# End of the first embedding: the first row tile turned by halves of its columns, two of its low parts ahead of the third gated product

## What is computed

```python
gate = jax.nn.sigmoid(rms_norm(h, g_ple[i]) @ ple_w_gate[i])      # p0: the embedding, i = 0
h = h + gate * (p[i] @ ple_w_proj[i])
h = h + FFN_HALF * swiglu(rms_norm(h, g_ffn1[i]), ffn1_w_in[i], ffn1_w_out[i])   # f2: i = 1
```

## Time and profile before

| | us |
|---|---|
| median of 3 runs | 1303.97 |
| lowest to highest | 1303.74 to 1305.53 |
| profiled execution, its own time | 1304.07 |
| its span on the core | 1302.3 |

### The profile page before, as it was taken

The page is one execution under the profiler, slowest core; times in us unless marked ns, Lnnn a source line. Parts: engine busy times, 40 slices in busy tenths (PEclk is TensorE's granted clock), DMA queues, the critical chain, the costliest instruction groups (busy, mean ns, idle before and its releaser), DMA issues.

```text
span 1302.3 us, 16738 instructions
## 1 busy us (share of the span) xinstructions
PE 1285.5 (99%) x6242; PEld 1058.6 (81%) x6242; DVE 929.1 (71%) x1295; ACT 678.7 (52%) x973; POOL 126.9 (10%) x190
## 2 busy tenths in 40 slices
PE   9999999999999999999999999999999999999997
PEld 6888888888888888888887777888888887788886
DVE  6878948986678956677875577667895656655674
ACT  6444537756444546644445567644444735566542
POOL 2000003712000000000001230000000133200000
PEclk9999999999999999999999999999999999999999
DMA  9765645228665554666564643466564496445541
GB/s 299 227 193 193 204 147 187 81 77 261 196 194 194 195 192 162 194 191 195 191 199 151 238 162 114 154 193 194 194 225 151 173 282 224 158 137 178 174 149 33
DMA packets 148673, 236.29 MB, mean 181 GB/s; under 512 B 10016, under 2 KB 103376, under 8 KB 148096
## 3 DMA queue, kind: packets, MB, share of 16 engines
q1 hardware_dynamic: 143600, 222.26, 52.4%
q0 software_dynamic: 4640, 12.81, 3.3%
q10 hardware_dynamic: 368, 0.37, 0.1%
HBM read 233.27 MB, written 4.47 MB: 183 GB/s over the span
## 4 chain that ended last, share of the span: by engine, by line
PE 91%; DVE 4%; ACT 3%; issue 1%; DMA 1%; SPq 0%; POOL 0%; POOLq 0%; DVEq 0%; ACTq 0%
PE acc L619 20%; PE acc L621 20%; PE acc L620 20%; PE acc L652 7%; PE acc L656 7%; PE acc L653 7%; PE misc L695 4%; DVE wl L2017 1%; ACT wh L1484 1%; PE misc L1289 1%; PE misc L836 1%; PE misc L1145 1%; DMA raw<-in_ffn_w_in_dram 1%; ACT xh L1528 0%; PE acc L816 0%
## 5 line engine op out<-in xcount | busy, mean ns | idle before, releaser
L2017 DVE TENSOR_TENSOR wl<-raw,wh 128x2048 fp32r<-128x2048 f32 (+2 forms) x200 | 452.7, 2270 | 183.4 <-ACT wh L1484 182.4
L1484 ACT ACTIVATE wh<-raw 128x2048 fp32r<-128x2048 f32 (+2 forms) x206 | 385.4, 1894 | 124.1 <-PE acc L656 104.3
L619 PE MATMUL acc<-wh,xh 128*128 128x512 f32 (+1 forms) x832 | 325.4, 391 | 2.6 <-ACT qf L1867 0.9
L621 PE MATMUL acc<-wh,xl 128*128 128x512 f32 (+1 forms) x832 | 322.9, 388 | 0.0
L620 PE MATMUL acc<-wl,xh 128*128 128x512 f32 (+1 forms) x832 | 322.7, 388 | 0.0
L619 PEld LDWEIGHTS acc<-wh,xh 128*128 128x128 f32 x832 | 156.3, 188 | 37.7 <-DVE wl L2005 3.2
L621 PEld LDWEIGHTS acc<-wh,xl 128*128 128x128 f32 x832 | 156.3, 188 | 31.9
L620 PEld LDWEIGHTS acc<-wl,xh 128*128 128x128 f32 x832 | 156.3, 188 | 31.1
L1567 ACT ACTIVATE sg<-acc,rstd 128x256 f32<-128x256 f32 x88 | 41.4, 475 | 242.7 <-PE acc L621 242.6
L2185 DVE STREAM_TRANSPOSE aT<-a_n 32x384 f32<-32x384 f32 (+1 forms) x256 | 137.2, 536 | 3.9
L652 PE MATMUL acc<-wh,ah 128*128 128x512 f32 x320 | 125.0, 391 | 0.0
(11 more groups left out here) (365 smaller groups left out, 1610.6 us busy)
## 6 DMA issues: line engine op xcount, KB each, us to landing
raw<-in_ffn_w_in_dram SPq DMA_DIRECT2D x172, 512.0 KB, 4.8
raw<-in_ffn_w_out_dram SPq DMA_DIRECT2D x88, 512.0 KB, 4.3
raw<-in_w_in_dram SPq DMA_DIRECT2D x64, 512.0 KB, 4.8
raw<-in_fox_w_in_dram SPq DMA_DIRECT2D x24, 512.0 KB, 4.3
raw<-in_ple_w_gate_dram SPq DMA_DIRECT2D x16, 512.0 KB, 4.2
raw<-in_mla_w_o_dram SPq DMA_DIRECT2D x8, 512.0 KB, 4.4
raw<-in_fox_w_o_dram SPq DMA_DIRECT2D x8, 512.0 KB, 4.4
raw<-in_w_out_dram SPq DMA_DIRECT2D x8, 512.0 KB, 4.4
```

The costliest lines, as they stand in the source:

```text
L619: pe.matmul(dst, hi, rhs_h, start=first, stop=False)
L621: return pe.matmul(dst, lo, rhs_h, start=False, stop=last)
L1484: act.activation(wh[:, s, 0:n], raw[:, s, 0:n], ACT.Copy).then_inc(hi_done, 1)
L2017: dve.tensor_tensor(wl[:, s, 0:n], raw[:, s, 0:n], wh[:, s, 0:n].bitcast(F32), ALU.subtract)\
```

## The change

Norm 4 (n4) takes the placing of n8 (k // 4 picks the bank). PE turns tile 0 of n4 by halves: the first half ahead of the last trio of the projection, waiting for the first quarter's sum alone (`h_half`, which p0's embed(0,0) now raises too), the second half behind that trio. Tile 1 is turned ahead of trio k = 7 in place of 6, by halves one straight after the other. DVE makes low parts 0 and 1 of tile 0 ahead of embed(1,0), the other six behind it. p1 counts `h_half` one further; its order is as before.

```diff
-            return (2 * t + k // 4, k % 4) if r == 8 else (2 * t + k % 2, k // 2)
+            return (2 * t + k // 4, k % 4) if r in (4, 8) else (2 * t + k % 2, k // 2)
...
-        TURN_AT = {"n1": 4}
+        TURN_AT = {"n1": 4, "n4": 7}
...
             def x_wait(name):
                 rd = PLAN[name][3]
-                return lambda t, k: pe.wait_ge(m_read[2 * t + k % 2], rd[2 * t + k % 2] + k // 2 + 1)
+                def wait(t, k):
+                    b, i = place(4 if name == "n4" else 0, k, t)
+                    pe.wait_ge(m_read[b], rd[b] + i + 1)
+                return wait
...
                         if t == 0 and k == TURN_AT.get(name, DK - 2):
                             rows_ready(pe, r, 1)
-                            turn_rows(name, 1)
+                            if name == "n4":
+                                turn_half(name, 1, 0)
+                                turn_half(name, 1, 1)
+                            else:
+                                turn_rows(name, 1)
...
                         for k in range(2):
-                            if t + n + k == 3 and after == "n8":
-                                pe.wait_ge(h_half, 1)
+                            if t + n + k == 3:
+                                pe.wait_ge(h_half, 1 if name == "p0" else 2)
                                 turn_half(after, 0, 0)
-                            elif t + n + k == 3:
-                                turn_h(after, r_after)()
...
             ple("p0", "n3", 3, "n4", 4)
+            rows_ready(pe, 4, 0)
+            turn_half("n4", 0, 1)
             ffn("f2", "n4", 4, "n5", 5)
...
-                    pe.wait_ge(h_half, 2)
+                    pe.wait_ge(h_half, 3)
                     turn_half("n8", 1, 0)
...
                     if n:
                         e.then_inc(h_added, 1)
-                    elif name == "p1":
+                    elif t == 0 or name == "p1":
                         e.then_inc(h_half, 1)
...
                 embed(0, 0)
                 embed(0, 1)
+                if after != "n8":
+                    rest_x(after, r + 1, 0, 0, 0)
+                    rest_x(after, r + 1, 0, 1, 1)
                 embed(1, 0)
...
                 else:
-                    rest(after, r + 1, 0)
+                    for k in range(2, DK):
+                        rest_x(after, r + 1, 0, k, k)
                     embed(1, 1)
                     rest(after, r + 1, 1)
```

## The result

| | before | changed |
|---|---|---|
| median of 14 runs, us | 1303.94 | 1307.26 |
| profiled execution | 1304.07 | 1307.26 |
| its span | 1302.3 | 1305.4 |

The ratio is 1.0025, with a 95% interval of 1.0018 to 1.0032: slower by 3.3 us. The forecast was 1307.3 us, with a range of 1305.9 to 1308.3.

The account below looks back on a forecast made before the run. PE's list of products plus its holes bounds the kernel. Head holes -0.88 us against 4.2 us of new holes and paced trios give +3.36: 1307.43 profiled, 0.10 less for the median, 1307.3 us; range 1305.9 to 1308.3.

Parts of the forecast that it names:

- The gain at the head: PE's holes of 0.58 us before turning tile 0 and 0.30 us before f2's first trio: at most 0.88 us gained.
- the first sum's cover of 0.81: Gated sum of columns 0 to 511 of tile 0 is done 0.81 us before PE wants to turn.
- The extra passage from transposes to products: Turning tile 0 by halves adds one more switch on PE from transposes to products, costing about 0.1 us.
- The round trip: ACT's high part and DVE's low part alternating over one misc bank: 0.79 us a step, against PE's 0.68.
- DVE's third sum: Tile 1's first-half sum between low parts 1 and 2 puts low part 2 at 516.20; fourth sum 2.2 us later.
- ACT between the tiles: Weights' high part, tile 0's square and its read-out put high part 0 of tile 1 at 522.42, before 520.43.
- The weights: Low part of f2's third weight group, behind tile 1's low parts, ends at 530.37; chunk 1 at 530.52, +3.4 us.
- Behind chunk 1: After chunk 1 of f2: later weights covered again, other waits cost nothing; nothing different but the shift.
- Rival 1: High and low parts keep their 0.39 us a step, so not slower: -0.35, 1303.6 us; chance 0.04.
- Rival 2: DVE reaches the third weight group 1.3 us sooner, so tile 1's fill ends last: +2.05, 1306.0 us; chance 0.12.
- Rival 3: PE's clock falls to its lower level in a hole: 5.4 us more for a tile's products, 1312.7; chance 0.03.
- Rival 4: Halves come no earlier, PE's first-half wait being on a count that comes with the second: +4.3, 1308.3; chance 0.02.

Follow-up runs that it names:

- the run with the order taken back: Changed kernel with DVE's third gated sum again ahead of all low parts of tile 0, halves and new banks kept: median 1306.90 us.
- the kernel with four banks: Changed kernel with k = 0 to 3 alternating between banks 0 and 1, k = 4 to 7 between banks 2 and 3: median 1303.27 us.

## Why the prediction was right

**The gain at the head** came a little larger: trio 0 at 514.30, forecast 514.5; the first sum's cover of 0.81 was real. "These 0.88 us are all that this change can give" counts holes only. Trio 0 came 0.98 earlier, because the two groups of four transposes and the trio between them took 1.54 us in all (512.76 to 514.30), where the eight and the trio had taken 1.62 (513.36 to 514.98). The extra passage from transposes to products, put at 0.1, shows no cost. It made no difference, as trio 2 waits for low part 2 in any case.

**The round trip** of 0.79 us held within 0.01 in every one of the steps over one bank, in both tiles (tile 0: 513.80, 514.59; 518.00, 518.79, 519.58; tile 1: 522.67, 523.46, 524.25, 525.03; 526.08, 526.86, 527.65), and the step at which the bank changes took 0.26, as forecast. It was the number on which all hung. Eleven round trips stand in the chain, five in tile 0 and six in tile 1, not the ten by which the lower bound was reckoned: that bound should have been 0.1 lower.

**DVE's third sum** put low part 2 at 516.18 (forecast 516.20) and, with the trips behind it, low part 7 at 519.58 (519.62) and the turning of tile 1 at 521.31 (521.34). The holes of PE were as forecast, 0.78 for 0.8 and 1.10 for 1.1.

**ACT between the tiles** was 0.14 off: high part 0 of tile 1 at 522.28, forecast 522.42. The term that I mis-sized is the read-out of the squares: ACT goes on 0.09 behind its start, not 0.19, which is its duration. The trace of before has this too: there the read-out of tile 1 starts at 524.26, and the next instruction at 524.36. The other 0.04 had come from tile 0, whose high part 7 was that much earlier (519.18 for 519.22).

**The weights** ended the chain as forecast, at 530.20 for 530.37. Chunk 1 started at 530.25 and not 530.52: 0.17 of the 0.27 came with low part 7 of tile 1 (527.65 for 527.82), 0.10 from the step between the weights' end and PE, which took 0.05 where I had 0.15.

**Behind chunk 1** nothing changed: 3.10 at chunk 1, 3.1 in the span.

**How near it came.** The mechanism was right, but that the total is off by 0.04 us only is in part luck. Chunk 1 was forecast 0.27 too late. Against that, the medians lie 3.32 apart and the profiled executions 3.19, more than the stage's 3.11, and the 0.10 that I took off for the median was not there in the changed kernel, whose median and profiled time are both 1307.26.

**The rivals.** Rival 1 (present pace) is refuted by the round trips; but the kernel with four banks is that rival made true, and there the stage gave 0.61 back, for which the forecast had 0.35. Rival 2 (only the fill counts) fell short: the fill would have ended at about 528.98, and PE waited for weights to 530.25. Taking that wait away gained only 0.36 since the work came back elsewhere. Rival 3: the clock stayed. In the busy times by stretch of the changed kernel (PE, PEld, DVE, ACT, POOL, then the granted clock) PE is busy in 12.21 of 14.90 us, and in 0.28 of 1.40 us in the hole ahead of chunk 1, and the clock is 1.00, the higher of its two levels:

```profile
515.30:530.20 14.90, 12.21 (x53) 8.36 (x51) 9.06 (x19) 9.91 (x20) 2.20 (x3) 1.00 0.15 49
528.90:530.30 1.40, 0.28 (x3) 0.05 (x1) 1.30 (x1) 1.40 (x1) 1.35 (x1) 1.00 0.00 0
```

The Trainium skill's page "TensorE: Matmul & The Clock Gate", section "Part 4: PE-mode transpose", says that transposes don't count as busy in the way products do; as the clock shows no fall here, no run shows it either way.

Rival 4: PE did start on the first half at 512.76.

What the prediction had not said is how little the third sum's new place matters by itself in the changed kernel (0.07). It counted the sum as a part of the delay, and the run with the order taken back shows that without it the chain begins as much later.

## What to carry to other kernels

Before a buffer is laid out anew so that its first half can be used sooner, look at who alternates over its banks: two engines that must take turns at a bank, as the waits of `round_x` make them, cost a full round trip a step (0.79 us here), two banks halve that, and whether the consumer notices depends on its own step (0.68 us, between the two). A layout that keeps both (halves over different pairs of banks) gave 0.61 us of the 0.88 that the halves had promised, and 0.97 once DVE's sums stood behind the low parts; 0.24 of these come with the placing alone. And a delay found at the end of an engine's queue mostly stays when the queue is reordered, if it has as much work in either place (0.92 of 1.27 us here); price the chain, not its last wait.

## What the runs showed of the hardware

An accumulator read-out on ACT lets the next instruction start 0.09 us behind its own start (522.19 to 522.28), though its row shows 0.19. A trio ahead of which PE stood idle takes 0.77 to 0.81 us in place of 0.68: in the changed kernel the first product of a trio released by a low part is followed after 0.34 (516.58 to 516.92 in its timeline), not 0.23. The instructions of a step (0.37 and 0.35) fill 0.72 of the 0.79 of a round trip, so the passing of two semaphores between ACT and DVE costs 0.07 us together, an estimate from these durations.
